# Retention and the projections of the short convolution in one interleaved order on TensorE

## The reference

```python
def short_conv_mixer(xin, b, c, z, conv_w, conv_b):
    u = jnp.pad(c * xin, ((0, 0), (CONV_K - 1, 0), (0, 0)))
    y = conv_b
    for j in range(CONV_K):                  # CONV_K = 3
        y = y + u[:, j:j + L] * conv_w[j]
    return b * y * jax.nn.silu(z)

def retention_mixer(q, k, v, z, ret_norm, cos, sin):   # 4 heads of 64
    ...
    s = jnp.einsum('bnchd,bnmhd->bnhcm', qc, kc) * intra_decay
    o_intra = jnp.einsum('bnhcm,bnmhd->bnchd', s, vc)
    ...
    o = rms_norm(o, ret_norm).reshape(B, L, RET_W)
    return o * jax.nn.silu(z)

def first_block(...):
    u = rms_norm(h, ln_w[l])
    (cx, cb, cc, cz, cq, ckv, krope, mz, rq, rk, rv, rz) = jnp.split(u @ w_in[l], IN_OFFSETS, axis=-1)
    y = concatenate([short_conv_mixer(cx, cb, cc, cz, ...), mla_mixer(...), retention_mixer(rq, rk, rv, rz, ...)])
    h = h + y @ w_out[l]                     # h[:, N_META:] goes on to the second block
```

## Time and profile before

| | us |
|---|---|
| median of three runs (2037.0 to 2038.58) | 2037.62 |
| the profiled execution | 2035.54 |
| its span, first to last instruction | 2033.8 |
| TensorE busy | 1817.5 |
| VectorE busy | 463.6 |
| ScalarE busy | 212.8 |

### The profile page before, as it was taken

The page is one execution under the profiler, slowest core; times in us unless marked ns, Lnnn a source line. Parts: engine busy times, 40 slices in busy tenths (PEclk is TensorE's granted clock), DMA queues, the critical chain, the costliest instruction groups (busy, mean ns, idle before and its releaser), DMA issues.

```text
span 2033.8 us, 20341 instructions
## 1 busy us (share of the span) xinstructions
PE 1817.5 (89%) x8256; PEld 764.8 (38%) x8256; DVE 463.6 (23%) x961; ACT 212.8 (10%) x421; POOL 15.1 (1%) x30
## 2 busy tenths in 40 slices
PE   7989999989998969998898898988988989889887
PEld 4545446433445533333233232332332323323322
DVE  2453436223346140110120120101201201012011
ACT  2041014001237110000000000000000000000000
POOL 0000000100000000000000000000000000000000
PEclk9899799999999979999999999999999999999999
DMA  6101020034120629999999999999999999999998
GB/s 229 52 9 54 29 83 1 0 120 133 42 83 1 284 98 426 424 425 425 425 425 425 425 425 425 425 426 425 425 426 425 425 425 426 425 425 425 426 425 343
DMA packets 82035, 598.53 MB, mean 294 GB/s; under 512 B 8824, under 2 KB 18168, under 8 KB 32712
## 3 DMA queue, kind: packets, MB, share of 16 engines
q1 hardware_dynamic: 81992, 597.93, 71.3%
HBM read 591.38 MB, written 2.10 MB: 292 GB/s over the span
## 4 chain that ended last, share of the span: by engine, by line
DMA 49%; PE 39%; SPq 6%; DVE 3%; ACT 2%; issue 1%; DVEq 0%; ACTq 0%
DMA arena<-in_w 48%; PE PS L1237 18%; PE PS L1706 6%; SPq L391 5%; PE PS L1620 3%; PE PS L1739 2%; PE PS L1537 1%; PE PS L1360 1%; PE PS L1420 1%; PE PS L1593 1%; PE PS L1676 1%; ACT arena L665 1%; PE PS L1450 1%; PE PS L1581 1%; PE PS L1434 1%
## 5 line engine op out<-in xcount | busy, mean ns | idle before, releaser
L1706 PE MATMUL PS<-arena 128*64 128x512 f32 (+1 forms) x3072 | 639.7, 562 | 112.6 <-DMA arena<-in_w 111.9
L1706 PEld LDWEIGHTS PS<-arena 128*64 128x64 f32 x3072 | 207.7, 136 | 545.0 <-issue 354.6
L1237 PE MATMUL PS<-arena 128*128 128x512 f32 (+6 forms) x1040 | 395.8, 540 | 3.2 <-DVE arena L1011 1.4
L1739 PE MATMUL PS<-arena 128*64 128x512 f32 x1408 | 325.2, 599 | 23.6 <-ACT arena L709 13.1
L1237 PEld LDWEIGHTS PS<-arena 128*128 128x128 f32 (+1 forms) x1040 | 188.8, 198 | 199.3 <-issue 190.5
L1739 PEld LDWEIGHTS PS<-arena 128*64 128x64 f32 x1408 | 114.6, 138 | 223.9 <-issue 170.0
L1202 DVE TENSOR_TENSOR arena<-arena,PS 128x1408 f32<-128x1408 f32 x16 | 25.9, 1621 | 699.2 <-PE PS L1706 699.2
L705 ACT ACTIVATE arena<-PS 128x1408 f32<-128x1408 f32 x16 | 21.5, 1345 | 742.8 <-PE PS L1706 742.8
L1211 DVE COPY arena<-PS 128x512 f32<-128x512 f32 x16 | 11.1, 691 | 329.1 <-PE PS L1739 329.1
L1753 PE MATMUL PS<-arena 64*128 64x512 f32 x256 | 76.7, 626 | 8.9 <-DVE arena L1196 8.1
L1219 DVE TENSOR_TENSOR arena<-arena,PS 128x512 f32<-128x512 f32 x128 | 77.9, 680 | 20.4 <-PE PS L1753 20.4
(11 more groups left out here) (245 smaller groups left out, 957.5 us busy)
## 6 DMA issues: line engine op xcount, KB each, us to landing
arena<-in_w SPq DMA_DIRECT2D x384, 1408.0 KB, 34.5
arena<-in_w_in SPq DMA_DIRECT2D x5, 2048.0 KB, 8.2
arena<-in_w_in SPq DMA_DIRECT2D x8, 1024.0 KB, 6.5
arena<-in_w_out SPq DMA_DIRECT2D x4, 2048.0 KB, 8.3
arena<-arena SPq DMA_DIRECT2D x64, 67.5 KB, 2.2
arena<-in_tab SPq DMA_DIRECT2D x1, 2304.0 KB
arena<-in_w_in SPq DMA_DIRECT2D x1, 2176.0 KB, 18.8
arena<-in_x SPq DMA_DIRECT2D x4, 512.0 KB, 6.4
```

The costliest lines, as they stand in the source:

```text
L1237: i = pe.matmul(dst, lhs(k), rhs(k), start=k == 0, stop=k == KD - 1)
L1706: i = pe.matmul(PS[64 * f:64 * f + 64, bank + c // 512, 0:w], XE[:, k, :], slot[:, f * FH + c:f * FH + c + w], start=k == 0, stop=k == KD ...
L1739: ins = pe.matmul(PS[64 * d:64 * d + 64, 6, :], HT[:, j, 64 * f:64 * f + 64], W2R[:, f, j, d * 512:(d + 1) * 512], start=f == 0 and j == 0 ...
```

## The change

The change touches all four of these:
- **Tokens in `UT`.** The meta tokens now lie in front of the 512 others (`ucol`), so the two early positions are adjacent to the first token. The c and x projections (now n = 4 to 7) read 514 columns in two halves of `LH` = 257, into two banks; the 2-column projections are gone.
- **Silu.** The retention gates and the conv gates no longer use the reciprocal: VectorE adds 1 (`silu_one`), ScalarE takes the logarithm and the exponent of its negative (`silu_sig`), VectorE multiplies (`silu_out`).
- **Order of the groups.** z and b are projected first (n = 0 to 3), c and x last.
- **Order on TensorE.** In the first five projections, a retention score is issued after every second slice, in two banks instead of four (`ret_score`). The value products and means stand between and inside later projections. The first two attention scores stand before the last two slices of projection 7. VectorE's and ScalarE's orders follow, and `conv_in(1)` comes after the first two row maxima.

The core of the diff:

```diff
-          ("w_in", [(C_CC, 256), (C_CX, 256)]), ("w_in", [(C_CZ, 256), (C_CB, 256)]),
+          ("w_in", [(C_CZ, 256), (C_CB, 256)]), ("w_in", [(C_CC, 256), (C_CX, 256)]),
...
+            def silu_sig(i, e):
+                act.wait_ge(s["sil_one"], i + 1)
+                own(act.activation(e, e, ACT.Ln))
+                own.settle()
+                act.activation(e, e, ACT.Exp, scale=-1.0).then_inc(s["sil_sig"], 1)
...
+            gate_sig(0), gate_sig(1)
+            ret_square(0), conv_copy(0)
+            ret_fac(0), ret_square(1)
+            ret_fac(1), conv_copy(1)
...
+            def silu_one(i, e):
+                dve.wait_ge(s["sil_exp"], i + 1)
+                dve.tensor_scalar(e, e, 1.0e18, 1.0, ALU.min, ALU.add).then_inc(s["sil_one"], 1)
+            def silu_out(i, e, z, dst):
+                dve.wait_ge(s["sil_sig"], i + 1)
+                return dve.tensor_tensor(dst, e, z, ALU.mult)
...
+            def conv_in(b):
+                dve.wait_ge(s["cc_evac"], b + 1)
+                dve.wait_ge(s["f_psum"], 6 + 2 * b)
+                u = CU1[:, b, :].rearrange("p (h c) -> p h c", h=2)
+                dve.tensor_tensor(u, u, PS[:, 4:6, 0:LH], ALU.mult).then_inc(s["cx_done"], 1)
...
+            for n in range(5):
+                for k in range(4):
+                    ret_decay(4 * n + k)
+                if n in (0, 2):
+                    silu_one(2 + n // 2, SCZ[:, n * 256:n * 256 + 512])
+                if n in (1, 3):
+                    conv_gate(n // 2)
+            ret_var(0), ret_norm(0)
+            conv_in(0)
+            ret_var(1), ret_norm(1)
...
             row_max(0), row_max(1)
+            conv_in(1)
...
+            def ret_score(i):
+                h, b = i // 5, i % 5
                 j, o = h // 2, 64 * (h % 2)
...
+                if i >= 2:
+                    pe.wait_ge(s["ret_s"], i - 1)
...
-            ret_scores(0)
-            pe.wait_ge(s["e_free"], 7)
-            ret_scores(1), ret_scores(2), ret_out(0), ret_scores(3), ret_mean(0), ret_out(1)
...
+            def conv_project(n, k):
...
+                if n >= 4:
+                    for h in range(2):
+                        i = pe.matmul(PS[:, 2 + 2 * (n % 2) + h, 0:LH], wg[:, k, blk:blk + P], UT[:, k, META - 2 + h * LH:META - 2 + (h + 1) * LH],
+                                      start=k == 0, stop=k == KD - 1)
+                else:
+                    i = pe.matmul(PS[:, n + 2, :], wg[:, k, blk:blk + P], UTX[:, k, :], start=k == 0, stop=k == KD - 1)
...
+            for n in range(8):
+                if n % 4 == 0:
+                    pe.wait_ge(ws_in[(4 + n // 4) % 2], ws_level[4 + n // 4])
+                if n in (4, 5):
+                    pe.wait_ge(s["cz_done"], n - 3)
+                if n == 6:
+                    pe.wait_ge(s["cc_evac"], 1)
+                if n == 7:
+                    pe.wait_ge(s["cx_done"], 1)
+                for k in range(KD):
+                    conv_project(n, k)
+                    if n < 5 and k % 2 == 1:
+                        ret_score(4 * n + k // 2)
+                    if n == 5 and k == 1:
+                        ret_mean(0)
+                    if n == 5 and k == 3:
+                        ret_out(1)
+                    if n == 6 and k == 3:
+                        ret_mean(1)
+                    if n == 7 and k == 5:
+                        pe.wait_ge(s["ro_v"], 2)
+                        scores(0), scores(1)
+                if n == 2:
+                    ret_out(0)
+                if n == 4:
+                    pe.wait_ge(s["ret_s"], 5 * RH)
+                    pe.wait_ge(s["e_free"], 7)
...
-            pe.wait_ge(s["cz_done"], 1)
+            pe.wait_ge(s["cc_evac"], 2)
+            scores(2), scores(3)
             pe.wait_ge(s["cx_done"], 2)
-            for i in range(4):
-                scores(i)
-            pe.wait_ge(s["cz_done"], 2)
+            pe.wait_ge(s["yr_ready"], 2)
```

More of the change, by code:

```diff
@@ L39 @@
 LT = S + META
+LH = (S + 2) // 2
 EPS = 1e-6
@@ L318, in toks, with ucol @@
             return (t * P, P) if t < NT else (S, META)
+        def ucol(t):
+            return META + t * P if t < NT else 0
+        UTX, UTM = UT[:, :, META:LT], UT[:, :, 0:META]
         block = ctx.enter_context(nc.Block())
@@ L538, in _, with ret_fac @@
                 act.activation(RV[0:n, t * 256:(t + 1) * 256], PS[0:n, [2, 7][(5 + t) % 2], 0:256], ACT.Copy).then_inc(s["rv_evac"], 1)
[L539 to L546, removed]
+            def silu_sig(i, e):
[3 more added lines that the diff above has]
+                act.activation(e, e, ACT.Exp, scale=-1.0).then_inc(s["sil_sig"], 1)
+            def ret_fac(j):
                 act.wait_ge(s["ro_v"], j + 1)
@@ L899, in _ @@
-            for j in range(2):
+            def silu_one(i, e):
[4 more added lines that the diff above has]
+                return dve.tensor_tensor(dst, e, z, ALU.mult)
+            for j in range(2):
+                e = SCR[:, j * 512:(j + 1) * 512]
+                silu_one(j, e)
+                silu_out(j, e, PS[:, [2, 7][j], :], SRZ[:, j * 512:(j + 1) * 512]).then_inc(s["e_free"], 1)
@@ L913, in _ @@
                 dve.tensor_tensor(z, RFAC[j], z, ALU.mult).then_inc(s["yr_ready"], 1)
[L915 to L925 removed]
+            dve.wait_ge(s["kT_psum"], 5)
+            dve.wait_ge(s["rrT_psum"], 5)
+            dve.wait_ge(s["e_free"], 7)
+            for n in range(5):
[8 more added lines that the diff above has]
+            ret_var(1), ret_norm(1)
             def conv_ops():
@@ L1350, in _ @@
                 ret_in(i)
-            def ret_scores(h):
+            def ret_score(i):
+                h, b = i // 5, i % 5
                 j, o = h // 2, 64 * (h % 2)
-                for b in range(5):
-                    i = 5 * h + b
-                    if i >= 4:
-                        pe.wait_ge(s["ret_s"], i - 3)
-                    c, n = toks(b)
-                    q0 = c if b < NT else 0
-                    pe.matmul(PS[0:n, i % 4, 0:S - q0], RKT[o:o + 64, j, c:c + n], RQT[o:o + 64, j, q0:S], start=True, stop=True)\
-                        .then_inc(s["rs_psum"], 1)
+                if i >= 2:
+                    pe.wait_ge(s["ret_s"], i - 1)
+                c, n = toks(b)
+                q0 = c if b < NT else 0
+                pe.matmul(PS[0:n, i % 2, 0:S - q0], RKT[o:o + 64, j, c:c + n], RQT[o:o + 64, j, q0:S], start=True, stop=True)\
+                    .then_inc(s["rs_psum"], 1)
             def ret_out(j):
```

123 lines of the change are left out of this document (53 added, 70 removed).

## The result

The changed kernel takes 2020.16 us (median of 4 runs, 2016.25 to 2021.53). The kernel before, run beside it, takes 2037.53 us (2037.0 to 2038.58). The ratio is 0.991, with a 95% interval of 0.9896 to 0.9923: **17.4 us faster**. Forecast were 2025.0 us, 12.6 us faster, in a range from 2018.5 to 2031.0. In a later group of runs the same two kernels gave 2020.92 against 2038.09, ratio 0.9912 (0.9895 to 0.9929).

The account below looks back on a forecast made before the run. TensorE bounds the part before the attention, by a 4.16 us wait for VectorE, then half clock. Terms summed to 85.5 us; with 1.75 handover the turn comes 12.6 us earlier, so 2037.62 becomes 2025.0 us, range 2018.5 to 2031.0.

Parts of the forecast that it names:

- Shape changes: TensorE, interleaved stretch: each of 20 scores pays two array-shape changes of 0.20 us, 8.0 us in all.
- Scores: TensorE, interleaved stretch: twenty retention scores, 3.11 us per head of five without the shape change, 12.4 us for four heads.
- Projections: TensorE, interleaved stretch: five projections of 512 columns take 34.35 us, three in halves of 257 columns take 20.8 us.
- The new wait: Before projection 5, TensorE waits 0.84 us for the last decay.
- Handover: From the last projection to the first turned probability in the attention: 1.75 us instead of 2.89.
- Value products: TensorE, interleaved stretch: two value products of 3.30 us each and 0.3 more in all for shapes at their edges, 6.9.
- The loss of 9.0 us: Half of the 18.0 us that TensorE ran at 1.2 GHz, from 206.4 to about 224.4; counted as regained.
- the step from the profiled execution to the median: Whole kernel: the profiled 2035.54 us and median 2037.62 have the same stages, so 12.6 us is subtracted from the median.
- Changes of shape for free: Rival, TensorE among long matmuls: the queue loads ahead, so shape changes cost nothing; gain 20.6 us, 2017.0 us; chance 0.08.
- One clock spell: Rival, new stretch: the granted clock falls once for about 20 us, costing 10 us, 2035.3 us; chance 0.07.
- Slower by two spells: Rival, interleaved stretch: two half-clock spells of 20.5 us cost 20.5 us, 2045.5 us; chance 0.04.
- Paced by decays: Rival, interleaved order: with two banks each of 18 scores waits about 0.7 us; 2037.6 us, no change; chance 0.04.

Follow-up runs that it names:

- the kernel with 128 rows: Changed kernel with every retention score contracting all 128 rows instead of its head's 64; start of the interleaved work to first turned probability 80.2 us, against 86.3.
- the kernel with pairs: Changed kernel with two retention scores behind the fourth and eighth slice of a projection, instead of one behind every second slice; stretch to the turn 83.1 us, against 86.3.
- the block kernels: Changed kernel with all 20 retention scores in one block: before the first conv projection, stretch to the turn 93.2 us; behind it, 79.5 us, median 2014.85 us.
- The kernel with the silu alone: Kernel before with only the retention gates computed by logarithm and exponent; first score to first turned probability 96.9 us, against 99.8.

## Why the prediction was right, step by step

**The stretch was right, to 1 us.** From the start of the interleaved work to the turn the sum had 87.2 (199.73 to 286.95); it took 86.3. The gain there was to be 12.6 and was 13.5. All but 0.1 of the difference lies before the last projection ends (85.5 said, 84.6 measured). The terms:
- Shape changes, 20 x 0.40 = 8.0: the boundary of 0.52 is the one of the earlier trace rows, and two kernels measured it by taking changes away (6.0 for 16 scores, 3.1 for ten pairs). Here lay the choice that mattered, since without them the forecast would have been 8.0 lower. The sum had 0.5 too much, since a 16-column score pays 0.31: 16 x 0.39 + 4 x 0.31 = 7.5. The rule that a change of tiling mode drains the engine (the Trainium skill, TensorEngine Tiling (Array Packing), section Key Properties) agrees with the trace. The rule gives no price.
- Scores, 12.4: without any change of shape a head's five take 0.85, 0.65, 0.43, 0.22 and 0.86 (the first four in the timeline of the kernel with 128 rows), 12.0 for four heads. The 3.31 from which the prediction took one change of 0.20 also held the change from 128 to 16 columns, about 0.1.
- Projections: the sum counted five of 512 columns and three in halves, but there are four of each. At 6.95 for one in halves (32 records of the 40 from 270.65 to 279.34) that is 0.1.
- The new wait: 0.77 measured, 0.84 said with the delay in front of the decay. All other decays stayed hidden, in the kernel with pairs as well.
- Handover: the turn came 1.62 behind the last projection, 1.75 said.
- Value products: 3.31 (229.47 to 232.78), said 3.30 and 0.15 for edges.
- The clock: 1.00 in the whole stretch. The loss of 9.0 us at half the clock behind the pause fits the block kernels: the same block at 0.50 behind a pause of 1.73, at 1.00 without one. The prediction's aside that without cover the whole 3.1 us of the gate would be a stall was too high for the stall (1.73) and left out the 11.6 that the clock then cost.

**What the sum did not have: 17.4 instead of 12.6.** The 4.8 missing are 0.9 of the stretch, 2.9 in front of it, -1.3 behind it, and 2.3 from the profiled pair (2035.54 and 2020.46) to the medians.
- In front: in the profiled pair the stretch itself began at 196.93 instead of 199.82. TensorE is at half speed twice early on in all kernels. In the first projection the records start 0.85 apart, and 0.43 only from 26.6 in before and from 24.5 in after (the clock column shows nothing there). A spell at 0.50 begins near 47 and lasted 23.9 us in before; in after it lasted 17.1, with another of 3.4 at 99.3. Half of 2.1 + 23.9 - 17.1 - 3.4 is 2.8, nearly all of the 2.9. Stretches of before and of after:

```profile
65.00:71.00 6.00, 6.00 (x10) 2.51 (x9) 0.69 (x6) 0.76 (x4) 0.00 (x0) 0.51 0.00 0
```

```profile
65.00:71.00 6.00, 6.00 (x15) 2.66 (x14) 0.00 (x0) 0.42 (x1) 0.00 (x0) 0.99 0.00 0
```

  The kernel with the silu alone, whose program up to there is that of before, shows 1.00 from 64.4 (its row above) and began at 196.41. The kernel with 128 rows, whose program up to there is that of after, shows 0.53 in the same stretch and began at 199.46:

```profile
65.00:71.00 6.00, 6.00 (x8) 2.34 (x8) 0.69 (x6) 0.56 (x4) 0.00 (x0) 0.53 0.00 0
```

  So either value comes with either program, a draw of each execution: the stretch began between 196.4 and 201.3 over all runs. That is enough to explain why the changed kernel's own executions lie up to 5 us apart. Whether the two medians drew alike in this part can't be told, since only profiled executions show it.
- Behind: the same matmuls come 16.4 us earlier than in before at the turn and to the end of the attention (337.67 and 354.08), 15.7 earlier at 469.15, 14.0 at 656.96, and 14.9 from the start of the experts (738.52) on. In between after spent 10.2 us at 0.50 near 400 where before spent 6.8, and 3.4 near 645 where before spent none. The prediction's range allowed for such dips. At the experts 0.9 comes back, and from there the end follows the front part, as it said.
- From the pair to the medians: before's profiled execution was 2.0 faster than the median beside after, after's 0.3 slower than its own. Its granted clock was 0.980, that of before's executions in the later groups 0.976 to 0.978. But the clock doesn't sort them: 2034.57 and 2039.11 both ran at 0.978. What made these 2.3 stays open, and with it whether the change has a part in them.

The term that was mis-sized is thus the last one, the step from the profiled execution to the median. It took over 12.6 unchanged, on the ground that both have the same stages; but the stages in front vary by several us from one execution to the next. That 17.4 still lies within the range owes something to luck: the stretch was forecast, the other 3.9 us were not.

**The rivals.** Changes of shape for free: refuted, each costs 0.20. The median alone could not have told: 2020.16 is nearer to this rival's 2017.0 than to the forecast of 2025.0. The stretch and the kernel with 128 rows decide it. One clock spell: didn't come here, but came in the kernel with the narrow projections put back, and cost 3.2. Slower by two spells: not seen. Paced by decays: not seen, and with pairs not either. The prediction missed a rival that was the best news of the case: grouped scores need few changes of shape, and heads on opposite rows run at once.

## What to carry to other kernels

Interleaving hides a stall, but on TensorE it has a price for each change of shape, here 0.20 us, and one projection in front of a block hid the same stall for fewer of them: put small matmuls of another shape in a few groups, just large enough that what frees their banks keeps up, sort them by shape, and alternate those that use opposite row halves. Count a pause on TensorE at the wait plus what follows at half the clock: here 4.2 us of wait were followed by a loss of 9.0, and shortening the wait to 1.7 saved little of that. Where the early part of a kernel has such spells of its own, compare stages between two events, not two profiled end times.

## What the runs showed of the hardware

- A change between tiles of 128x128 and 64x128 costs 0.20 us, on either side (gaps of 0.52 and 0.53 between record starts instead of 0.43; 0.39 less for a score that stays at 128 rows). Between 128x128 and 128x16 both changes together cost 0.31 (4.60 against 4.29).
- Two matmuls on opposite 64 rows run at once, with full 512 columns and different banks: 0.70 us for both, 0.69 for one. That tiles operate independently is in the same list of the Trainium skill (TensorEngine Tiling (Array Packing), section Key Properties). The trace agrees, and all it took here was to put the two next to each other in the program. The value products, on two 64-column halves, do so in before already: their first 16 records take 2.30 (230.35 to 232.65), where 4.3 would be the estimate for one behind the other at the gaps between equal shapes (0.43, 0.32, 0.22 and 0.11, four of each).
- The granted clock fell to 0.50 behind two pauses of 1.73 us among scores of 64 rows, 0.7 and 0.4 us after TensorE was at work again, and stayed there for 23.9 and 17.1 us. In the pause of 4.16 it fell while TensorE stood still, at 204.0, for 20.5. It also fell with TensorE busy throughout, behind 2-column matmuls, for 6.8. A pause of 0.77 between a score and a projection left it at 1.00:

```profile
254.00:283.20 29.20, 28.07 (x134) 21.70 (x133) 11.67 (x21) 4.55 (x10) 0.00 (x0) 1.00 0.02 2
```

- How long the early spell lasts differs from execution to execution, with the program up to there the same: 17.1 us in eight of the profiled ones, 20.5 in one, 23.9 in the other five. With it the start of the stretch moves by about 3 us.
